# A decoder step with retrieved experts: the start of its first stream is rearranged (top-k of head groups as asides between the dots, scores in pairs, second trunk from pick 36)

## The chip, the cores and the metric

The kernel runs on one core of one Trainium2 chip. The metric is the device time of one execution in microseconds (us). A core has a matrix engine (TensorE, PE in the profile), a vector engine (VectorE, DVE), an engine for activations (ScalarE, ACT), GpSimd (POOL) and SyncE (SP). Each runs its own list of instructions in order. They wait for each other through semaphores, and 16 DMA engines move the data.

## The reference, cut to what matters

Two groups of tokens (512 prompt tokens and 8 sequences of 8 tokens) pass through two layers. A layer adds a mixer, a cross attention and a retrieval of experts ("PEER") to its input. Everything is float32. Only the last part matters for the change:

```python
q = einsum('td,de->te', t, w_pq).reshape(T, 8, 2, 128)        # 8 heads, two halves of a query
s = einsum('thpk,hpnk->thpn', q, sub_keys)                     # 128 scores for each half
s1, i1 = top_k(s[:, :, 0], 16);  s2, i2 = top_k(s[:, :, 1], 16)
cand = s1[..., :, None] + s2[..., None, :]                     # sums of the best of both halves
top_s, pos = top_k(cand, 16)                                   # 16 experts of 16384, for each head
g = softmax(top_s)
a = gelu(einsum('td,ted->te', t, peer_u[idx]))                 # a dot product with each expert's u row
out = einsum('te,ted->td', g * a, peer_v[idx])                 # a weighted sum of the v rows
```

Each token takes 128 experts (8 heads of 16), and each expert has a u row and a v row of 4 KB. The rows are gathered from memory.

## The kernel before

**Passes and picks.** Tokens lie in five tiles: four of 128 tokens, one of 64. A pass is one layer over one group of tiles: passes 0 and 2 take tiles 0 and 1, passes 1 and 3 take tiles 2 to 4. Each pass has a *trunk* (mixer, attention, queries and scores of the retrieval) and a *stream* of *picks*. A pick is one expert for each of the 128 tokens of a tile: one gather of 128 u rows (0.52 MB) and one of 128 v rows. Pass 0 has 256 picks (128 for each tile, head by head, 16 to a head), pass 1 has 320, and there are 1152 picks in all. While the stream of one pass runs, the trunk of the next pass is computed beside it.

**The order of the work.** It is fixed at build time by *steps*. Step m of the stream does the dot product of pick m (VectorE, `dot`, line 1793) and, `LAG` = 8 steps later, its weighted sum. The sum of a pick is done on VectorE (`sum_up`, line 1809) or on TensorE, as a product with a diagonal matrix of weights (line 1057); the first 40 picks of pass 0 are all summed on TensorE. `places` gives each trunk job the step at which it is due (`AHEAD`) and after which it may begin (`STARTS`). On each engine a function `peer_to(n)` first does all of that engine's stream work up to step n. TensorE calls it at the end of each job, with the next job's `STARTS`, and does the sums of picks m with m + 8 < n there. ScalarE calls it before it empties a job's result out of PSUM, and makes there, four picks at a time, gelu, weight (which needs the head's softmax factor, `gate`) and the diagonals. VectorE calls it before each piece of trunk work.

**GpSimd's queue** (`gather`, line 989) issues the gathers in one order. There are 8 buffers for u rows and 8 for v rows. The u row of pick m waits for the dot of pick m-8 and for its head's indices (`idx_done`). The v row of pick v waits for the sum of pick v-8. Before: the u rows of picks 0 to 7, then one wait for the attention's last product (its weights lie in the v buffers), then the v rows 0 to 7 in a burst, then u rows 8 to 15 alone, and from pick 16 on the u row of pick m and the v row of pick m-8 by turns.

**The start of the first stream.** Tile 0 of pass 0 is asked head by head. `first_tail` computes the queries and scores of heads 0 and 1 for both tiles, and the queries of head 2. After that the remaining columns of the query projection (jobs `pq`, two to a head, line 1084) and the scores (jobs `sc`, line 1399) follow in the order pq 6, 7, sc 2, pq 8, 9, sc 3, and so on to sc 7, with the steps 5, 11, 15, 19, 24, 29 for sc 2 to 7. The weights of `pq` come in four units of 2 MB into two slots, each loaded by SP when the unit before it in the slot is spent. SP loads the vectors of pass 1 (`PAR` and others) once sc 7 is done.

`top_group(0, k)` finds the experts of group k of the heads on VectorE; the groups are heads 0 | 1 | 2, 3 | 4, 5 | 6, 7. It has nine parts, and between two parts `breathe` calls `peer_to`, which spreads the dots over the group's window of steps. The windows are (0, 0), (0, 11), (11, 19), (19, 29), (29, 40). All five are run in line: VectorE waits at the start of each group for ScalarE to have copied its scores, and does no dot while it waits. Part 8 ends with the indices (line 1927). After part 9 `weigh_group` normalises the `gate` of the group before. `top_k(p, i)` for the other tiles runs as an *aside*: `peer_to` looks after each step whether the next part is due (`aside_to`). The trunk of pass 1 begins on all engines at step `FIRST` = 40 and is spread evenly to step 200.

Of the kernel before, what the change touches and what calls it, by code (L numbers as in the profile page):

```python
# [42 lines left out]
BLK = 4  # L43
# [9 lines left out]
FIRST = 40  # L53
HEAD = 40
# [87 lines left out]
def first_tail():  # L142

    jobs = [(at[:-1], "dve" if at[0] == "xo" else "act", 2 if at[0] in ("xo", "sk", "n") else 1, 1) for at in FIRST_TAIL]
    for h in range(2, PH):
        jobs += [(("pq", c), "act", 1, 1) for c in queries_before(h)] + [(("sc", h), "act", 2, 1)]
    return jobs
# [102 lines left out]

def places(p):
# [4 lines left out]
    if p == 0:  # L256
        score = {("sc", h): (0, 0, 5, 11, 15, 19, 24, 29)[h] for h in range(PH)}
# [5 lines left out]
    begin, end = step_base(p - 1) + (FIRST if p == 1 else LAG + 2), step_base(p)  # L263
# [179 lines left out]
def decoder_step(nc, A, O):  # L443
# [21 lines left out]
    with ExitStack() as ctx:  # L465
# [312 lines left out]
        def head_window(p, k):  # L778

            ends = [AHEAD[p, "sc", h + n - 1] for h, n in head_groups(p)] + [FIRST if p == 0 else step_base(p) + CARRY if carries(p) else step_base(p) - OVER]  # L780
# [186 lines left out]
        def _(pool):  # L967
# [31 lines left out]
            for m in range(STEPS_IN_ALL):  # L999
                if m == NU:  # L1000
                    pool.wait_ge(job_done, JOB[0, "xo", 1] + 1)
                    for v in range(NV):
                        gather_values(v)
# [6 lines left out]
                if m >= LAG + NV:  # L1010
# [4 lines left out]
        def _(pe):  # L1015
# [186 lines left out]
            def trunk(p):  # L1202
# [188 lines left out]
                for h in range(0 if p else 2, PH):  # L1391
                    for c in queries_before(h):
# [18 lines left out]
        def _(act):  # L1411
# [52 lines left out]
            asides += [(step_base(1) - 8, copy_beside, ())]  # L1464
            asides.sort(key=lambda a: a[0])
# [64 lines left out]
            def trunk(p):  # L1530
# [55 lines left out]
                n = ncols(g)  # L1586
                if p:
                    act.wait_ge(idx_done, turns_to(p - 1, len(GROUPS[(p - 1) % 2]) - 1 if g == 0 else 0))
                for a in range(2):
                    for c in range(BLK * a, BLK * a + BLK):  # L1590
                        evac((p, "c", c), F1[:, c, 0:n], pf((p, "c", c)))
                    for c in range(BLK * a, BLK * a + BLK):
                        evac((p, "u", c), F2[:, c, 0:n], pf((p, "u", c)), ACT.Gelu_apprx_tanh)
# [123 lines left out]
                for h in range(0 if p else 2, PH):  # L1717
                    for c in queries_before(h):
# [8 lines left out]
                    for k, (h0, some) in enumerate(head_groups(p)):  # L1727
                        if k and h == h0 + some - 1:
                            group_exps(p, k - 1)
                k = len(head_groups(p)) - 1  # L1730
                peer_to(head_window(p, k)[1] - 1)
                group_exps(p, k)
# [13 lines left out]
        def _(dve):  # L1746
# [95 lines left out]
            asides, going = [(p, i) for p in range(2 * DEPTH) for i in range(1, len(GROUPS[p % 2]))], []  # L1842

            def aside_to(n):

                while asides:
                    p, i = asides[0]
                    if not going:
                        going.append([0, top_k(p, i)])
                    k, work = going[0]  # L1850
                    if topk_steps(p, i, k) > n:
# [145 lines left out]
            def top_group(p, k):  # L1997
# [3 lines left out]
                first, after = head_window(p, k)  # L2001
                at = [0]

                def breathe():
                    at[0] += 1
                    peer_to(first + round((after - first) * at[0] / SEGS))

# [15 lines left out]
                breathe()  # L2023
# [4 lines left out]
                breathe()  # L2028
                each(lists, lambda a: dve.max_index(i16[:, a, 8:16], m16[:, a, 8:16], part[a]))
                candidates(all_cand, h, n)  # L2030
                breathe()
                each(heads, lambda a: dve.max(tops[:, a, 0:8], cand[a]))
                each(heads, lambda a: dve.max_index(pos[:, a, 0:8], tops[:, a, 0:8], cand[a]))
                breathe()
                each(heads, lambda a: dve.match_replace(cand[a], tops[:, a, 0:8], cand[a], LOWEST))
                each(heads, lambda a: dve.max(tops[:, a, 8:16], cand[a]))
                breathe()
# [3 lines left out]
                breathe()  # L2041
                marks = mark_table(S[0][:, h * 256:(h + n) * 256])
                ch.link(mark_places(marks, h, n))
                breathe()
                ch.link(mark_keys(marks, h, n))
                breathe()
# [3 lines left out]
                breathe()  # L2050
                if k and not carries(p):
                    weigh_group(p, k - 1)

            def trunk(p):
# [41 lines left out]
                peer_to(AHEAD[p, "par"])  # L2096
                for part in range(len(norm_parts(p, 0))):
# [203 lines left out]
                for i in range(nt):  # L2301
# [4 lines left out]
                    if i and not p:  # L2306
                        top_group(0, 0)
# [7 lines left out]
                for k in range(0 if p else 1, len(head_groups(p))):  # L2315
                    top_group(p, k)
                weigh_group(p, len(head_groups(p)) - 1)
# [47 lines left out]
```

## Time and profile before

| | us |
|---|---|
| time before, median of 3 runs (4105.68 to 4110.06) | 4108.83 |
| the profiled execution | 4111.88 |
| its span in the trace | 4110.0 |
| GpSimd busy / VectorE busy / TensorE busy | 2604.4 / 2929.3 / 3273.3 |

The span runs from the first to the last instruction, and 1.88 us of the profiled execution lie around it. The span has two parts. Up to 436.71 us the trunk of pass 0 runs alone. From there to the end the gathers run without a break of more than some 15 us. In the windows below, "DMA share" is the mean busy share of 16 DMA engines (1.03 is what a full stretch shows), and GB/s is what they moved.

### The profile page before, as it was taken

Reading aid. Unit: us, or ns where it says so; the run is one execution under the profiler, and the core shown is the slowest. Engines: PE = TensorE matmul, PEld = TensorE weight load, DVE = VectorE, ACT = ScalarE, POOL = GpSimd, SP = SyncE. Lnnn points to the kernel's source line nnn. Section 1 sums busy time; section 2 is a strip of 40 time slices with the busy share of each in tenths; the row PEclk is TensorE's granted clock in tenths of the full one; section 3 lists DMA queues with packets and bytes.
Section 4 is the critical chain, followed back from the end, with each engine's and each line's share of the span. In section 5 each row is a group of like instructions: output and inputs, shape, how many; then the busy total and the mean of one; then the engine's idle time right before and its main releaser. Section 6 shows DMA issues by size and latency. Waiting matters only on the chain. (4 is left out here: it accounts for less than half of the span.)

```text
span 4110.0 us, 37140 instructions
## 1 busy us (share of the span) xinstructions
PE 3273.3 (80%) x11224; PEld 1943.7 (47%) x11224; DVE 2929.3 (71%) x5930; ACT 1011.5 (25%) x2939; POOL 2604.4 (63%) x2318
## 2 busy tenths in 40 slices
PE   9999989898789788875848769897868866756666
PEld 6876646665546235664335426564635422212211
DVE  2110589988667878887776789997868776676754
ACT  1001331122422322122223421121313222321233
POOL 0000476676567677787777776777647777777775
PEclk9999999999889899887878969898879989988876
DMA  5445799999999999999999999999999999999998
GB/s 214 153 144 194 261 344 386 377 397 406 377 391 407 384 402 405 402 404 407 410 404 395 407 373 377 404 403 406 409 403 367 393 409 409 407 411 409 409 410 347
DMA packets 462382, 1522.37 MB, mean 370 GB/s; under 512 B 41220, under 2 KB 45604, under 8 KB 462184
## 3 DMA queue, kind: packets, MB, share of 16 engines
q0 software_dynamic: 331776, 1208.11, 74.9%
q1 hardware_dynamic: 130408, 311.90, 20.2%
q8 instruction: 91, 1.49, 0.1%
q14 instruction: 107, 0.88, 0.1%
HBM read 1512.62 MB, written 7.23 MB: 370 GB/s over the span
## 5 line engine op out<-in xcount | busy, mean ns | idle before, releaser
L989 POOL DMA_INDIRECT urow<-in_peer_u_dram,idx x1152 | 1323.3, 1149 | 1051.4 <-DVE idx L1927 440.8
L989 POOL DMA_INDIRECT vrow<-in_peer_v_dram,idx x1152 | 1278.8, 1110 | 437.5 <-issue 316.3
L1057 PE MATMUL ps<-vrow,diag 128*128 128x512 f32 (+1 forms) x2068 | 987.7, 694 | 393.8 <-DMA vrow<-in_peer_v_dram,idx 344.9
L1084 PE MATMUL ps<-RH,W 128*128 128x256 f32 (+1 forms) x4544 | 1174.5, 420 | 120.2 <-DMA W<-in_w_in_dram 46.2
L1084 PEld LDWEIGHTS ps<-RH,W 128*128 128x128 f32 x4544 | 892.0, 198 | 409.9 <-issue 96.3
L1793 DVE CUSTOM_DVE_ANT_0 urow<-urow,T 128x1024 f32<-128x1024 f32 x712 | 869.5, 1224 | 200.4 <-DMA urow<-in_peer_u_dram,idx 152.3
L1809 DVE SCALAR_TENSOR_TENSOR X<-vrow,wts,X 128x1024 f32<-128x1024 f32 x590 | 759.3, 1287 | 114.9 <-issue 95.8
L1057 PEld LDWEIGHTS ps<-vrow,diag 128*128 128x128 f32 (+1 forms) x2068 | 332.1, 195 | 998.5 <-issue 792.3
L1793 DVE CUSTOM_DVE_ANT_0 urow<-urow,ps 128x1024 f32<-128x1024 f32 x376 | 456.4, 1218 | 282.4 <-DMA urow<-in_peer_u_dram,idx 277.8
L1488 ACT ACTIVATE gel<-dots 128x4 f32<-128x4 f32 x288 | 59.0, 205 | 1782.3 <-DVE dots L1793 1759.0
L1084 PE MATMUL ps<-RB,W 128*128 128x256 f32 (+1 forms) x1024 | 253.4, 408 | 6.8 <-DVE RV L2232 3.1
L1506 ACT ACTIVATE diag<-ident,wts 128x128 f32<-128x128 f32 (+1 forms) x645 | 224.5, 372 | 127.3 <-PE ps L1057 123.3
L1490 ACT ACTIVATE wts<-gel,gate 128x1 f32<-128x1 f32 x1152 | 245.1, 283 | 9.3
L1084 PEld LDWEIGHTS ps<-RB,W 128*128 128x128 f32 x1024 | 195.3, 191 | 62.5 <-DVE RV L2232 3.5
L1106 PE MATMUL ps<-W,RV 128*128 128x512 f32 (+1 forms) x320 | 130.9, 613 | 54.1 <-DVE RV L2232 54.1
L1106 PE MATMUL ps<-W,RB 128*128 128x512 f32 (+1 forms) x384 | 162.1, 619 | 4.8 <-DVE RB L2155 3.1
L1106 PE MATMUL ps<-W,RH 128*128 128x512 f32 (+1 forms) x320 | 132.2, 610 | 17.4 <-DVE RH L2084 16.3
L1106 PEld LDWEIGHTS ps<-W,RV 128*128 128x128 f32 (+1 forms) x320 | 54.4, 186 | 128.6 <-issue 73.2
L1488 ACT ACT_TABLE_LOAD x76 | 97.5, 1283 | 66.1 <-issue 52.4
L1106 PEld LDWEIGHTS ps<-W,RB 128*128 128x128 f32 (+1 forms) x384 | 67.6, 190 | 96.9 <-issue 92.4
L1528 ACT ACTIVATE RB<-ps 128x256 f32<-128x256 f32 (+2 forms) x130 | 51.0, 418 | 249.4 <-PE ps L1084 221.1
L1528 ACT ACTIVATE RV<-ps 128x320 f32<-128x320 f32 (+4 forms) x110 | 47.9, 447 | 261.5 <-PE ps L1084 202.4
(271 smaller groups left out, 2309.0 us busy)
## 6 DMA issues: line engine op xcount, KB each, us to landing
W<-in_w_in_dram SPq DMA_DIRECT2D x56, 2048.0 KB, 18.6
W<-in_w_pq_dram SPq DMA_DIRECT2D x16, 2048.0 KB, 18.8
urow<-in_peer_u_dram,idx POOLq DMA_INDIRECT x1152, 15.1
vrow<-in_peer_v_dram,idx POOLq DMA_INDIRECT x1152, 15.2
W<-in_w_a_out_dram SPq DMA_DIRECT2D x8, 2048.0 KB, 19.1
W<-in_w_b_out_dram SPq DMA_DIRECT2D x8, 2048.0 KB, 19.2
W<-in_w_mix_o_dram SPq DMA_DIRECT2D x8, 2048.0 KB, 14.1
W<-in_w_xq_dram SPq DMA_DIRECT2D x8, 2048.0 KB, 18.9
```

Source lines behind the costliest of these rows:

```text
L989: return pool.indirect_dma_start(ring[:, slot, :], None, table, bass.IndirectOffsetOnAxis(ap=idx[:, q % TSLOT, e:e + 1], axis=0))
L1057: o = pe.matmul(out, diag[:, pe_turn[m] % NDIAG, 0:rows], vrow[:, m % NV, b * 512:(b + 1) * 512], start=m in pe_first, stop=m in pe_last)
L1084: m = pe.matmul(pf(name), slot(u)[:, k, c % BLK * P:c % BLK * P + P], src[:, k, 0:ncols(name[0] % 2)], start=(k == 0), stop=(k == KC - 1))
L1106: m = pe.matmul(out, src[:, k, i * P:i * P + rows], row_slot((p, kind, n))[:, k % 4, a * 512:(a + 1) * 512], start=(k == 0), stop=(k == KC ...
L1488: ch.link(act.activation(gel[:, :], dots[:, at, :], ACT.Gelu_apprx_tanh))
L1490: w = act.activation(wts[:, at, j:j + 1], gel[:, j:j + 1], ACT.Copy, scale=gate[:, q % TSLOT, e + j:e + j + 1])
L1506: made = act.activation(diag[part, pe_turn[m] % NDIAG, 0:rows], ident[part, part], ACT.Copy, scale=wts[part, m // GRP % WRING, m % GRP:m % ...
L1528: act.activation(out, in_, func).then_inc(act_evac, 1)
L1793: dve.tensor_tensor_reduce(urow[:, m % NU, :], urow[:, m % NU, :], rows, 1.0, 0.0, ALU.mult, ALU.add, dots[:, n % WRING, m % GRP:m % GRP + ...
L1809: dve.scalar_tensor_tensor(out=out, in0=vrow[:, m % NV, :], scalar=wts[:, m // GRP % WRING, m % GRP:m % GRP + 1], in1=base, op0=ALU.mult, ...
```

## The change

The change does six things. All but the last two concern the steps 0 to 46 of pass 0.

1. The groups 2, 3 and 4 of tile 0 become asides with windows of their own; the groups 0 and 1 stay in line. Group 1's window ends at step 8 (was 11).
2. The query columns come four at a time before two heads' scores: pq 6, 7, sc 2, sc 3, pq 8 to 11, sc 4, sc 5, pq 12 to 15, sc 6, sc 7. The scores' steps become 5, 5, 12, 12, 18, 18, so that TensorE has fewer sums to do ahead of them.
3. GpSimd issues u and v rows by turns from pick 8 on.
4. ScalarE's exponentials of a group become asides too, and the last group's gate is normalised at its own end.
5. The window of `top_k` of tile 1 moves from steps (40, 104) to (46, 106).
6. The trunk of pass 1 begins at step `SECOND` = 36 instead of 40. VectorE waits there for sc 7 to have been copied. The end of the trunk's stretch (step 200) stays.

```diff
+SECOND = 36
+FIRST_WINDOWS = ((0, 0), (0, 8), (12, 23), (23, 34), (34, 44))
+INLINE = 2
...
-    return step_base(p) + FIRST, step_base(p) + FIRST + WIDE
+    return step_base(p) + FIRST_WINDOWS[-1][1] + 2, step_base(p) + FIRST + WIDE + 2
...
+def queries_of(p, h):
+    if p:
+        return queries_before(h)
+    return () if h % 2 else tuple(range(2 * h + (2 if h == 2 else 0), 2 * h + 4))
...
-        score = {("sc", h): (0, 0, 5, 11, 15, 19, 24, 29)[h] for h in range(PH)}
+        score = {("sc", h): (0, 0, 5, 5, 12, 12, 18, 18)[h] for h in range(PH)}
...
-    begin, end = step_base(p - 1) + (FIRST if p == 1 else LAG + 2), step_base(p)
+    begin, end = step_base(p - 1) + (SECOND if p == 1 else LAG + 2), step_base(p)
...
             for m in range(STEPS_IN_ALL):
-                if m == NU:
+                if m == LAG:
                     pool.wait_ge(job_done, JOB[0, "xo", 1] + 1)
-                    for v in range(NV):
-                        gather_values(v)
...
-                if m >= LAG + NV:
+                if m >= LAG:
                     gather_values(m - LAG)
...
+            asides += [(first + (after - first) * 6 // SEGS + 1, group_exps, (0, k)) for k, (first, after) in enumerate(FIRST_WINDOWS) if k]
...
+            asides[:0] = [(0, -k) for k in range(INLINE, len(FIRST_WINDOWS))]
+            def aside_steps(p, i, k):
+                if i > 0:
+                    return topk_steps(p, i, k)
+                first, after = FIRST_WINDOWS[-i]
+                return first + round((after - first) * k / SEGS)
...
-                breathe()
+                yield
...
+                if p == 0 and k == len(FIRST_WINDOWS) - 1:
+                    weigh_group(p, k)
+            def heads_inline(p, k):
+                first, after = head_window(p, k)
+                for at, part in enumerate(top_group(p, k)):
+                    peer_to(first + round((after - first) * (at + 1) / SEGS))
...
+                if p == 1:
+                    await_evac(dve, LAST_SC[0])
```

## Rows read from the trace of the kernel before

**Rows 1.** The page: DMA's share in 40 slices; the sums on VectorE (busy, mean ns).

```profile
DMA 5445799999999999999999999999999999999998
...
L1809 DVE SCALAR_TENSOR_TENSOR X<-vrow,wts,X 128x1024 f32<-128x1024 f32 x590 | 759.3, 1287 | 114.9 <-issue 95.8
```

**Rows 2.** Windows: stretch, its length, PE, PEld, DVE, ACT, POOL busy, PEclk, DMA share, GB/s.

```profile
440.00:545.00 105.00, 90.43 (x392) 66.32 (x392) 67.08 (x232) 32.75 (x98) 59.68 (x56) 0.95 0.97 360
545.00:656.00 111.00, 101.56 (x319) 50.68 (x318) 92.46 (x262) 35.43 (x98) 88.64 (x73) 0.97 0.97 356
656.00:870.00 214.00, 200.86 (x749) 141.51 (x749) 210.33 (x442) 36.66 (x106) 137.12 (x111) 0.95 1.00 381
...
860.00:880.00 20.00, 17.71 (x66) 12.24 (x66) 18.23 (x25) 6.21 (x14) 16.57 (x12) 1.00 1.03 403
```

**Rows 3.** Waits of POOL, 440 to 545 us: for whom, us in total, times, longest.

```profile
POOL vrow L989 <- PE ps L1057: 23.8, 7, 5.8
POOL urow L989 <- DVE idx L1927: 7.2, 1, 7.2
```

**Rows 4.** Timeline of POOL: start, us, instruction, [idle before it, and its releaser].

```profile
468.92 0.94 POOL L989 DMA_INDIRECT urow<-in_peer_u_dram,idx  x1 [0.30 <-issue]
...
484.57 0.94 POOL L989 DMA_INDIRECT vrow<-in_peer_v_dram,idx  x1 [5.79 <-PE ps L1057]
...
526.86 0.94 POOL L989 DMA_INDIRECT vrow<-in_peer_v_dram,idx  x1 [3.64 <-PE ps L1057]
...
537.62 1.07 POOL L989 DMA_INDIRECT vrow<-in_peer_v_dram,idx  x1 [0.30 <-issue]
...
544.71 0.94 POOL L989 DMA_INDIRECT vrow<-in_peer_v_dram,idx  x1 [4.77 <-PE ps L1057]
```

**Rows 5.** Timeline of VectorE around the indices of head 1.

```profile
455.39 1.23 DVE L1793 CUSTOM_DVE_ANT_0 urow<-urow,T 128x1024 f32<-128x1024 f32 x1
...
472.34 1.23 DVE L1793 CUSTOM_DVE_ANT_0 urow<-urow,T 128x1024 f32<-128x1024 f32 x1 [15.71 <-DMA urow<-in_peer_u_dram,idx]
...
476.66 0.17 DVE L1927 SCALAR_TENSOR_TENSOR idx<-RB 128x16 uint32<-128x16 uint16 x1
```

**Rows 6.** Timeline of TensorE from pq 8 on (a job's matmuls are recorded twice).

```profile
469.06 8.83 PE L1084 MATMUL ps<-RH,W 128*128 128x256 f32 x32 [2.75 <-DMA W<-in_w_pq_dram]
...
482.35 5.39 PE L1057 MATMUL ps<-vrow,diag 128*128 128x512 f32 x12 [3.56 <-ACT diag L1506]
487.57 7.07 PE L1084 MATMUL ps<-RH,W 128*128 128x256 f32 x32
...
540.39 0.34 PE L1073 MATMUL ps<-ident,PAR 48*128 48x48 f32 x1 [6.04 <-DMA PAR<-in_conv_w_dram]
540.66 24.94 PE L1057 MATMUL ps<-vrow,diag 128*128 128x512 f32 x52
```

**Rows 7.** Timeline of ScalarE: the wait for head 0's gate, and a group's exponentials.

```profile
478.33 1.28 ACT L1488 ACT_TABLE_LOAD   x1 [12.50 <-DVE gate L1995]
...
485.07 1.28 ACT L1426 ACT_TABLE_LOAD   x1
486.37 0.31 ACT L1426 ACTIVATE gate<-tops,gneg 128x16 f32<-128x16 f32 x1
```

**Rows 8.** Windows, columns as in rows 2: three thinner stretches of the DMA.

```profile
600.00:620.00 20.00, 20.00 (x55) 8.16 (x54) 18.70 (x45) 2.11 (x10) 15.97 (x14) 1.00 0.93 328
800.00:820.00 20.00, 17.75 (x56) 12.22 (x57) 19.48 (x35) 4.06 (x8) 13.51 (x10) 0.79 0.84 297
...
1040.00:1080.00 40.00, 32.09 (x203) 25.74 (x201) 31.55 (x44) 23.45 (x48) 17.51 (x14) 0.87 0.86 337
```

**Rows 9.** Timeline of SP's queue from 600 us: the weight loads of pass 1.

```profile
618.14 147.23 SPq L951 DMA_DIRECT2D W<-in_w_in_dram  x9
```

**Rows 10.** Waits of all engines, 1000 to 1100 us.

```profile
DVE rmax L2257 <- PE ps L1300: 18.3, 1, 18.3
...
PE ps L1073 <- DVE RB L2076: 6.8, 1, 6.8
```

More of the change, by code:

```diff
@@ L145, in first_tail @@
     for h in range(2, PH):
-        jobs += [(("pq", c), "act", 1, 1) for c in queries_before(h)] + [(("sc", h), "act", 2, 1)]
+        jobs += [(("pq", c), "act", 1, 1) for c in queries_of(0, h)] + [(("sc", h), "act", 2, 1)]
     return jobs
@@ L778, in head_window @@
         def head_window(p, k):
-            ends = [AHEAD[p, "sc", h + n - 1] for h, n in head_groups(p)] + [FIRST if p == 0 else step_base(p) + CARRY if carries(p) else step_base(p) - OVER]
+            if p == 0:
+                return FIRST_WINDOWS[k]
+            ends = [AHEAD[p, "sc", h + n - 1] for h, n in head_groups(p)] + [step_base(p) + CARRY if carries(p) else step_base(p) - OVER]
             return ends[k], ends[k + 1]
@@ L1391, in trunk @@
                 for h in range(0 if p else 2, PH):
-                    for c in queries_before(h):
+                    for c in queries_of(p, h):
                         project((p, "pq", c), c, hT)
@@ L1586, in trunk, with evac_gated @@
                 n = ncols(g)
+                def evac_gated(some):
+                    for c in some:
+                        evac((p, "u", c), F2[:, c, 0:n], pf((p, "u", c)), ACT.Gelu_apprx_tanh)
                 if p:
@@ L1591, in trunk @@
                         evac((p, "c", c), F1[:, c, 0:n], pf((p, "c", c)))
-                    for c in range(BLK * a, BLK * a + BLK):
-                        evac((p, "u", c), F2[:, c, 0:n], pf((p, "u", c)), ACT.Gelu_apprx_tanh)
+                    evac_gated(range(BLK * a, BLK * a + BLK))
                 if g:
@@ L1717, in trunk @@
                 for h in range(0 if p else 2, PH):
-                    for c in queries_before(h):
+                    for c in queries_of(p, h):
                         evac((p, "pq", c), qp[c // 2 % 3][:, c % 2, 0:n], pf((p, "pq", c)))
@@ L1727, in trunk @@
                     for k, (h0, some) in enumerate(head_groups(p)):
-                        if k and h == h0 + some - 1:
+                        if p and k and h == h0 + some - 1:
                             group_exps(p, k - 1)
-                k = len(head_groups(p)) - 1
-                peer_to(head_window(p, k)[1] - 1)
-                group_exps(p, k)
+                if p:
+                    k = len(head_groups(p)) - 1
+                    peer_to(head_window(p, k)[1] - 1)
+                    group_exps(p, k)
             for p in range(2 * DEPTH):
@@ L2314, in trunk @@
                     dve.sem_inc(row_spent, 1)
-                for k in range(0 if p else 1, len(head_groups(p))):
-                    top_group(p, k)
-                weigh_group(p, len(head_groups(p)) - 1)
+                for k in range(0 if p else 1, len(head_groups(p)) if p else INLINE):
+                    heads_inline(p, k)
+                if p:
+                    weigh_group(p, len(head_groups(p)) - 1)
             ch.mark(dve.memset(eps[:, :], EPS))
```

27 lines of the change are left out of this document (11 added, 16 removed).

## The prediction

> **What bounds the kernel now.** I read the page first, then the windows, the waits of GpSimd, and the timelines of the first 110 us of the stream.
>
> The page shows no engine above 80% busy, but the DMA engines stand at full share in nearly every slice after the fourth [rows 1]. A full stretch shows a share of 1.03 and 403 GB/s [rows 2]. The bytes are fixed, so after the stream's start the end moves only by what the DMA leaves unused. I count that as (403 - rate)/403 of a stretch. It is 11.2 us in 440 to 545 (360 GB/s), 12.9 us in 545 to 656 (356) and 11.7 us in 656 to 870 (381) [rows 2]. Later there are 6.6 us in 1040 to 1080 (337) [rows 8]. The change touches nothing else, since passes 2 and 3 keep their steps.
>
> Each of these stretches has its own limit. In 440 to 545 GpSimd waits 23.8 us in 7 waits for TensorE's sums, and 7.2 us once for VectorE's indices [rows 3]. In 545 to 656 it issues 73 gathers, two to a step: 111/36.5 = 3.04 us a step. In 656 to 870 VectorE is busy for 210.33 of 214 us [rows 2].
>
> **The wait for head 1's indices goes (edit 1, with 3).** Before, group 1's window of 11 steps puts dots 8 and 9 ahead of the indices. Dot 8 waits 15.71 us for its row, because the v rows 0 to 7 were queued ahead of it, so the indices come at 476.66 [rows 5] and GpSimd idles 7.2 us for them [rows 3]. Now only dots 0 to 6 stand ahead. Dot 7 is done at 456.6 [rows 5], so the indices come at about 458 and the gate of head 0 at about 459. The u row of pick 16 goes out at 470, when the 24 gathers ahead of it are issued [rows 4]. Taken alone that is worth 7 us.
>
> **What is late next (edit 2).** The next gather is v row 8, and it needs sum 0. Before, sum 0 follows sc 3; now it follows sc 4. ScalarE's 12.50 us wait for the gate goes too [rows 7], but it was not last: TensorE is held by its own products. I count from 469.06, where the weights of pq 8 arrive; that load is not moved. Pq 8 and 9 take 8.83, pq 10 and 11 another 6.9 (one pair is 7.07 with its tail), sc 4 1.05: 485.8 [rows 6]. Sum 0 takes 1.8 (5.39/3) and v row 8 goes at 487.9, against 484.57 [rows 4]. Between sum 0 and sum 3 ScalarE now makes head 1's exponentials and switches its table twice (1.28 + 0.5 for the first [rows 7], 1.28 + 1.1 for gelu and weights), so sum 3 ends at 493.3 instead of 491.3 or so.
>
> Now the queue behind: sc 5 to 494.3, pq 12 to 15 in 13.9 to 508.2, sc 6 to 509.2, and only then sums 4 to 9 (10.8) to 520.0, sc 7 to 521.0. So v row 12 waits from about 497 to 511, a stall of 14 us where before there were several of 4 to 6. Behind v row 12 stand all later u rows in GpSimd's queue. SP loads `PAR` after sc 7, and TensorE stood 6.04 us for it [rows 6]: 527.1, against 540.39. From there to the gather that the first sum releases took 4.3 us before (540.39 to 544.71) [rows 6, 4], which gives v row 18 at 531.4. Four pairs of gathers took 537.62 - 526.86 = 10.76, or 2.69 a pair [rows 4], so v row 24 goes at 531.4 + 6 x 2.69 = 547.5. Before it went at 544.71 [rows 4].
>
> The start of the stream therefore brings **+2.8 us**. The removed index wait is eaten by the sums. The bounds are -11.2 (the DMA full throughout) and +16.1 (the third rival).
>
> A rule of the Trainium skill (ScalarE: Activation LUTs, What ACT_TABLE_LOAD costs) puts a switch of the table at 1.28 us plus 1.38 us of drain. The trace shows 485.07 to 486.37, so 1.30 to the next instruction [rows 7], and no drain. By the page sum 3 would end up to 2.8 us later. Nothing else hangs on that.
>
> **The head groups as asides, ScalarE's exponentials, VectorE's wait for sc 7.** The same instructions run, the same number of times. Dots no longer wait for ScalarE's copies. But GpSimd waited for a dot nowhere in 440 to 545 [rows 3], so this is free, and bounded by the 12.9 us that lie unused in the next stretch. I take 0. Sc 7 is done 35 us ahead of step 36, so the new wait costs nothing.
>
> **The trunk of pass 1 from step 36.** Four steps of 3.04 us are 12.2 us; less the 2.8 the trunk starts 9.4 us earlier. Its first weight load after the two already there is at 618.14 [rows 9] and comes at about 608.7. In 600 to 620 the DMA leaves 3.7 us unused (328 GB/s) [rows 8], of which 11.3/20 lie behind 608.7: **-2.1 us** (bounds 0 and -3.7).
>
> From 656 VectorE sets the pace. At step s the trunk is now at (s - 36)/164 of its way instead of (s - 40)/160, which is 2.1% further at step 62 (the step near 656 us). The stretch has 55.5 steps of about 2.5 us for a dot (1.23 [rows 5]) and a sum (1.29 [rows 1]), so some 70 us of VectorE's 210 are trunk and tile 1's top-k, over 37% of the trunk's way. 2.1% of 70/0.37 is 4.0 us that is already done when VectorE becomes the limit. I take **-3.5**, near that end, because VectorE has 3.7 us of slack in all [rows 2]. The bounds are -5, and +3 where tile 1's top-k, two steps later, falls on the trunk's gating; the thinnest stretch, 297 GB/s in 800 to 820, leaves 5.3 us [rows 8].
>
> At 1046 VectorE stands 18.3 us for the attention scores [rows 10], and this makes the 6.6 us unused in 1040 to 1080. It lies in TensorE's products between the second norm and the scores, and before them TensorE waits 6.8 us for VectorE's norm [rows 10]: a head start of TensorE ends in that wait. The steps between are 2.5% more per product. I take **-1** (bounds -6.6 and +1).
>
> The sum is +2.8 - 2.1 - 3.5 - 1.0 = -3.8. The profiled execution took 4111.88 (its span of 4110.0 and 1.88 around it), which gives 4108.1. It stands 3.05 above the median of the runs, so against that median I forecast 4108.8 - 3.8 = 4105.0.
>
> **The rivals.** *The start is fed after all.* If v rows 8 to 17 are not held by sums 0 to 9 (pq 8 to 11 quicker, or loads of weights filling the gap), the 11.2 us go in full: -11.2 - 2.1 - 1 = -14, or 4094.5. For it: 31 us of GpSimd's idle time in that stretch [rows 3], and the loads of pass 1's first weights come forward by 11 us, since the first of them waits for pq 11. Against it: TensorE is busy 90.43 of 105 us [rows 2], and no product goes.
>
> *The head start carries through.* TensorE and its weight loads are the trunk's limit right up to the scores, the norm's 6.8 us wait notwithstanding, and the 18.3 us wait shrinks by 9: -6.6 in place of -1, so -9.4, or 4099.4. For it: TensorE is busy 94% of 656 to 870 [rows 2]. Against it: that wait of 6.8.
>
> *Slower: the ring of v rows starves.* Each microsecond by which the sum after `PAR` is later than 527 holds GpSimd for a microsecond, because v row 18 and everything behind it wait. If sc 7 or the load of `PAR` comes no earlier than before (TensorE at its lower clock, as in pq 8 and 9, or `PAR` queued behind the second weight load), v row 18 goes at 544.7 and v row 24 at 560.8: +16.1 in place of +2.8. The loads of pass 1's weights fill some of such a gap, so I take half way, +9.4, for its price, and 4108.8 + 9.4 = 4118.2 where the earlier trunk then brings nothing. It decides from a `PAR` transposition later than 530, where the term reaches +5.7 and outweighs the later ones but for 1 us. For it: TensorE's order puts six sums behind four products, and the stall near 500 is certain to come. Against it: TensorE had 12.4 us of waits in that stretch (2.75, 3.56 and 6.04 [rows 6]), and one of them goes.
>
> *It does nothing.* The terms cancel, VectorE's relief falls where the DMA is full anyway (1.03 in 860 to 880 [rows 2]): 4108.8.
>
> **How the numbers follow.** About 8 us (0.2%) is what a measurement can tell from no change. Forecast 0.43 (its own range 4101 to 4109), start fed 0.19, head start carries 0.13, starved 0.19, nothing 0.06. Faster by over 8.2 us (below 4100.6): the first rival, two thirds of the second and a rest of the forecast, 0.19 + 0.09 + 0.05 = 0.33. Slower: most of the third and a rest of the others, 0.19. The same: 0.48. The range of 4092 to 4117 takes in the first rival and reaches to the third; it leaves out 0.1 on either side.
>
> **What would show it.** Right: GpSimd's wait for `idx` near 477 is gone; v row 8 goes at about 488; one long stall ends near 511; sc 7 near 521, `PAR`'s transposition near 527, v row 24 between 545 and 550; the load of 618.14 near 609; the 18.3 us wait before 1046 nearly as long. Wrong: DMA above 385 GB/s in 440 to 545, or that wait under 12 us (faster rivals); `PAR` transposed after 530 or a new wait of GpSimd for `idx` (slower). The prediction fails as a whole if the time leaves the range, or if it moves by stretches behind 1250 us, which the change doesn't touch.

## The result

The changed kernel takes 4120.92 us (median of 12 runs, 4116.86 to 4125.27), the kernel before on the same chip 4109.49 (12 runs, 4104.11 to 4119.41). The ratio is 1.0029, with an interval of 1.0022 to 1.0036. So it is slower by some 11 us, where 4 us faster were forecast, and it lies above the range. The profiled execution took 4119.95 with a span of 4117.9, 7.9 longer than before.

**The start of the stream came nearly as predicted.** Of GpSimd's timeline, the gathers that waited, up to 545 us (start, us, instruction, idle before it):

```profile
487.68 0.94 POOL L1001 DMA_INDIRECT vrow<-in_peer_v_dram,idx  x1 [16.74 <-PE ps L1067]
...
510.26 0.94 POOL L1001 DMA_INDIRECT vrow<-in_peer_v_dram,idx  x1 [12.96 <-PE ps L1067]
...
529.98 0.94 POOL L1001 DMA_INDIRECT vrow<-in_peer_v_dram,idx  x1 [4.00 <-PE ps L1067]
```

Of TensorE's timeline, score 7 and the transposition of `PAR`, and of SP's queue the weight load that stood at 618.14:

```profile
518.41 1.05 PE L1409 MATMUL ps<-KV,RV 128*128 128x128 f32 x8
525.66 0.34 PE L1083 MATMUL ps<-ident,PAR 48*128 48x48 f32 x1 [6.20 <-DMA PAR<-in_conv_w_dram]
```

```profile
614.10 21.32 SPq L963 DMA_DIRECT2D W<-in_w_in_dram  x2
```

The wait for `idx` [rows 3] is gone, v row 8 goes at 487.68 (487.9 predicted), the long stall ends at 510.26 (511), and `PAR` is transposed at 525.66 (527.1).

**The loss stands at 656 to 700 us.** The windows of the kernel after (stretch, length, busy time of PE, PEld, DVE, ACT and POOL, PEclk, DMA share, GB/s); the first three lines answer to the first three of [rows 2], the fourth to the first of [rows 8]:

```profile
440.00:545.00 105.00, 95.50 (x393) 69.09 (x394) 61.92 (x218) 33.38 (x102) 56.37 (x53) 0.93 0.91 344
545.00:656.00 111.00, 100.32 (x322) 50.01 (x320) 82.42 (x223) 32.59 (x84) 75.31 (x69) 0.97 0.97 366
656.00:870.00 214.00, 201.29 (x745) 141.77 (x745) 208.93 (x472) 35.76 (x102) 135.43 (x110) 0.96 0.95 360
...
600.00:620.00 20.00, 20.00 (x54) 7.83 (x53) 15.12 (x39) 0.85 (x4) 9.57 (x9) 1.00 0.81 294
...
656.00:700.00 44.00, 44.00 (x159) 30.77 (x159) 42.54 (x112) 2.11 (x10) 18.93 (x14) 0.96 0.77 286
670.00:680.00 10.00, 10.00 (x39) 7.04 (x38) 9.47 (x20) 0.00 (x0) 3.31 (x3) 1.00 0.36 119
```

The window from 656 to 700 of the kernel before:

```profile
656.00:700.00 44.00, 44.00 (x166) 31.17 (x166) 42.71 (x105) 2.11 (x10) 18.06 (x15) 0.96 1.00 384
```

Counted as in the prediction, (403 - rate)/403 of the stretch, 44 us at 286 GB/s leave 12.8 us unused and at 384 GB/s 2.1: 10.7 us more, in one hole. The other stretches add up to little. The first 105 us lose 4.2 more (344 against 360). The next 111 gain 2.8 (366 against 356), and 656 to 870 as a whole loses 11.2 (360 against 381). That is 12.6. Less the 2.85 by which the first gather went earlier (433.86 against 436.71) it is 9.7. The change did not bring these 2.85: a second trace of the kernel before (e9) has its first gather at 434.15. The u row of pick 256, far behind all this, went out at 1368.9 against 1360.3, 8.6 us late. The spans differ by 7.9, so little is given back or lost after it.

The clock of TensorE is no part of it: the granted clock is 0.96 in 656 to 700 in both kernels, and 1.00, its upper level, in the 56 us ahead.

**What makes the hole.** Waits of VectorE, 545 to 720 us (for whom, us in total, times, longest), after:

```profile
DVE bns L2152 <- ACT RV L1578: 11.2, 2, 10.5
DVE urow L1809 <- PE ps L1130: 9.2, 1, 9.2
```

and before, the wait of the same place:

```profile
DVE urow L1793 <- PE ps L1120: 4.6, 1, 4.6
```

L1578 is ScalarE's gelu of the v projection, L1130 (before, L1120) the spread of lg and lb on TensorE. Spread after and before, in TensorE's timelines:

```profile
652.36 3.83 PE L1130 MATMUL ps<-GV,ident 16*128 16x128 f32 x32
```

```profile
653.82 3.83 PE L1120 MATMUL ps<-GV,ident 16*128 16x128 f32 x32
```

VectorE's consumer of the spread is due three picks earlier (58 for lg instead of 61), and VectorE comes to it 6.1 us earlier (654.45 - 9.25 = 645.20, against 655.91 - 4.59 = 651.32, from its timelines). TensorE has it ready only 1.5 us earlier. The reason stands in TensorE's timeline of the v projection (L1116), which began 7.8 us earlier (589.29 against 597.11) and ended 0.6 earlier (635.01 against 635.61):

```profile
589.29 5.39 PE L1116 MATMUL ps<-W,RH 128*128 128x512 f32 x12 [2.57 <-DVE RH L2109]
594.52 1.88 PE L1067 MATMUL ps<-vrow,diag 128*128 128x512 f32 x4
596.23 3.60 PE L1116 MATMUL ps<-W,RH 128*128 128x512 f32 x8
...
619.25 1.88 PE L1067 MATMUL ps<-vrow,diag 128*128 128x512 f32 x4
620.96 14.05 PE L1116 MATMUL ps<-W,RH 128*128 128x512 f32 x40
634.94 17.49 PE L1094 MATMUL ps<-RH,W 128*128 128x320 f32 x64
```

TensorE takes the row sums up to step 48 (`head_steps`). With the trunk begun at 36, six of them fall between the products of the v projection, at 1.72 us each (594.52 to 596.23); before there were two. Those four take 6.9 of the 7.8 us. VectorE now stands 10.5 us for the gelu (to 625.65) and 9.2 for the spread (to 654.45).

GpSimd waits for the sums that now lie in the projection as well, four times between 604 and 622 us, where before it waited for nobody from 600 to 656. The DMA ran at 294 GB/s in 600 to 620 (328 before [rows 8]). Of GpSimd's waits, 600 to 656 us:

```profile
POOL vrow L1001 <- PE ps L1067: 10.3, 4, 3.3
```

While VectorE stands for the spread it makes no dot, so no u row comes free, and GpSimd waits again (timeline of GpSimd, 648 to 676 us):

```profile
648.83 0.94 POOL L1001 DMA_INDIRECT vrow<-in_peer_v_dram,idx  x1 [0.30 <-issue]
655.95 1.74 POOL L1001 DMA_INDIRECT urow<-in_peer_u_dram,idx  x1 [6.18 <-DVE dots L1809]
...
662.42 1.18 POOL L1001 DMA_INDIRECT vrow<-in_peer_v_dram,idx  x1 [0.30 <-issue]
674.23 1.74 POOL L1001 DMA_INDIRECT urow<-in_peer_u_dram,idx  x1 [10.63 <-DVE dots L1809]
```

The second wait is VectorE's product with lg and lb, nine instructions without a dot. It was there before too (9.26 us), but then the buffers were full when it began: six gathers had gone out in the 9.5 us before the wait, now four in 14 us. Two stands in a row empty the queues, and 119 GB/s at 670 to 680 is the result (406 before).

### The profile page after: what moved, and what is told of

It reads as the page before. It is cut to its first block and busy times, and to the rows that moved or that the text cites. A ratio compares the mean times of both kernels' runs of the same rounds, so it can differ in the third digit from the quotient of the medians.

```text
span 4117.9 us, 37139 instructions
## 1 busy us (share of the span) xinstructions
PE 3266.8 (79%) x11224; PEld 1935.1 (47%) x11224; DVE 2930.0 (71%) x5930; ACT 1012.1 (25%) x2939; POOL 2602.7 (63%) x2318
## 5 line engine op out<-in xcount | busy, mean ns | idle before, releaser
L1116 PE MATMUL ps<-W,RV 128*128 128x512 f32 (+1 forms) x320 | 131.8, 616 | 62.7 <-DVE RV L2259 62.7
L1116 PE MATMUL ps<-W,RB 128*128 128x512 f32 (+1 forms) x384 | 159.5, 612 | 6.2 <-DVE RB L2182 3.1
L1116 PE MATMUL ps<-W,RH 128*128 128x512 f32 (+1 forms) x320 | 130.4, 602 | 18.8 <-DVE RH L2109 18.3
L1116 PEld LDWEIGHTS ps<-W,RV 128*128 128x128 f32 (+1 forms) x320 | 54.7, 187 | 137.8 <-issue 73.7
L1116 PEld LDWEIGHTS ps<-W,RB 128*128 128x128 f32 (+1 forms) x384 | 66.5, 187 | 96.7 <-issue 91.3
L1809 DVE CUSTOM_DVE_ANT_0 urow<-urow,RV 128x1024 f32<-128x1024 f32 x64 | 78.2, 1225 | 43.5 <-DMA urow<-in_peer_u_dram,idx 41.2
## 6 DMA issues: line engine op xcount, KB each, us to landing
W<-in_w_mix_o_dram SPq DMA_DIRECT2D x8, 2048.0 KB, 14.3
```

What stands on the lines that cost most here:

```text
L1116: m = pe.matmul(out, src[:, k, i * P:i * P + rows], row_slot((p, kind, n))[:, k % 4, a * 512:(a + 1) * 512], start=(k == 0), stop=(k == KC ...
L1809: dve.tensor_tensor_reduce(urow[:, m % NU, :], urow[:, m % NU, :], rows, 1.0, 0.0, ALU.mult, ALU.add, dots[:, n % WRING, m % GRP:m % GRP + ...
```

## The experiments

Each was timed in five rounds beside the kernel before. The first eight ran on two chips that took 3% longer for every kernel (4231.64 and 4246.88 us for the kernel before; DMA 374 to 376 GB/s in 3000 to 4000 us against 403), with more scatter: the time from the u row of pick 256 to the end, which the change doesn't touch, was between 2857 and 2877 us in their traces, and between 2747 and 2752 in all the others. The others ran where the kernel before took 4110 to 4112. So the sizes come from the later ones. The rate in brackets is the DMA's at 656 to 700 us. "After" is the changed kernel.

**The first batch: one part at a time.** e1 is after with

```diff
-SECOND = 36
+SECOND = 40
```

> The changed kernel with the trunk of pass 1 from step 40 again; all edits of steps 0 to 46 stay. Theory A (the trunk's due steps lie 4 steps earlier than TensorE can follow, so VectorE stands 10.5 us for the gelu of v and 9.2 us for the spread lg, lb, where before it stood 4.6): the long wait for the gelu goes, the wait for lg/lb falls under 6 us, DMA in 656 to 700 us is back above 370 GB/s (286 in the changed kernel), and the time falls by 6 to 10 us, to 0.1% of the kernel before. Rival B (the head of the stream costs it: v row 24 is 3.5 us later counted from the first gather, and VectorE without its backlog runs into the same waits anyway): the waits stay within 3 us of the changed kernel's, the time stays 0.2 to 0.3% above before.

e2 is after with VectorE's steps alone put off:

```diff
-                return AHEAD[name] + {"v": LATE_GELU, "oa": ...
+                return AHEAD[name] + {"v": LATE_GELU + 3, "lg": 3, "lb": 3, "oa": ...
```

> The changed kernel, trunk still from step 36, but VectorE takes v, lg and lb of pass 1 three steps later (steps 56, 61 and 63 in place of 53, 58 and 60); no other engine's list changes. Theory A: VectorE does dots while TensorE finishes, the two waits shrink from 19.7 us in all to under 10, and the time falls by 5 to 9 us. Rival B: no change, 0.2 to 0.3% above before. Rival C (TensorE is late because six sums in place of two now lie within its projection of v, and everything after it is late too): VectorE only waits later, at the short convolution, and under 3 us come back.

e3 is the kernel before with the trunk's start alone:

```diff
-    begin, end = step_base(p - 1) + (FIRST if p == 1 else LAG + 2), step_base(p)
+    begin, end = step_base(p - 1) + (36 if p == 1 else LAG + 2), step_base(p)
```

> The kernel before with the trunk of pass 1 planned from step 36; VectorE still runs the groups to step 40 in line, with nothing else of the change. Theory A: the cost comes with it, 0.12 to 0.3% slower than before, with VectorE's waits for the gelu of v and for lg/lb over 12 us in all. Theory D (it takes both: 36 hurts only where VectorE has no backlog of dots): within 0.1% of before. Rival B: within 0.05%.

e4 is after with the scores of one head at a time, as before:

```diff
-        score = {("sc", h): (0, 0, 5, 5, 12, 12, 18, 18)[h] for h in range(PH)}
+        score = {("sc", h): (0, 0, 5, 11, 15, 19, 24, 29)[h] for h in range(PH)}
-    return () if h % 2 else tuple(range(2 * h + (2 if h == 2 else 0), 2 * h + 4))
+    return queries_before(h)
```

> The changed kernel with the order of queries and scores of before (pq two at a time, scores at steps 5, 11, 15, 19, 24, 29) and the trunk from 36. The sums of the first picks come earlier: v row 8 near 477 in place of 487.7 us, no stall of GpSimd over 8 us behind it. If the head's cost of 3.5 us at v row 24 passes through, the time falls by 3 to 4 us against the changed kernel. If PAR is late again as before (540), v row 24 is where it was before and the waits of theory A shrink too, since TensorE's lateness is then shared by the stream: 0.1 to 0.2% above before. If nothing of the head passes through, it stays at 0.29%.

Measured: e1 1.0032 [1.0021, 1.0044], e2 1.0021 [1.0011, 1.0031], e3 1.0024 [1.0009, 1.0039], e4 1.0016 [1.0003, 1.0029]. e3 shows that the start from 36 makes a kernel slower without anything else of the change. Its trace has the same two waits as after and 289 GB/s at 656 to 700, on a trunk that is otherwise the old one:

```profile
DVE bns L2125 <- ACT RV L1567: 12.2, 1, 12.2
DVE urow L1793 <- PE ps L1120: 12.1, 1, 12.1
```

e1 seems to speak against this: its trace has no wait for the gelu and the u rows up to pick 80 go out 12 us earlier than in after, yet its median is as bad. But its traced execution was the fastest of its eight, at 4233.59 us, 2 us above the median of the kernel before on that chip. The trace shows no loss because that execution had hardly any. What the other seven lost, and where, is open.

e2 does not decide. Its ratio lies between what theory A and rival C asked for, its interval overlaps that of after, and its trace still has a wait of 7.3 us ahead of a dot and 326 GB/s at 656 to 700. In e4 v row 8 goes at 478.61, near the 477 expected, but both waits stay as in after (10.0 and 9.2 us) and so does the rate behind them (285 GB/s). What the start of the stream gains there does not reach the hole.

**The second batch: a control, the start of the trunk on the other side, the two parts together.** e5 is the changed kernel as it is, e6 is e1 again, e7 has `SECOND = 44`, and e8 is e4 with `SECOND = 40`.

> The changed kernel again, beside the kernel before, as the control of the following three. All theories: 0.22 to 0.36% slower than before; the u row of pick 70 is issued about 27 us later than before, counted from the first gather, and that of pick 256 about 11.

> The trunk from 40 again, as in e1, whose trace showed the early loss gone (u row of pick 70 at 225 us after the first gather, before 224, changed 251) while its time was no better. Theory A: the time is 0.1 to 0.25% below the control's. Rival E (what the early stretch gives is lost again later, where the DMA limits): equal to the control within 0.05%, and the u row of pick 256 is no earlier than in the control.

> The changed kernel with the trunk of pass 1 from step 44. Theory A: VectorE's waits for the gelu and for lg/lb shrink further (under 5 us in all), the u row of pick 70 comes at 222 us or less after the first gather, and the time lies 0.2 to 0.35% below the control's, so within 0.1% of before. Rival F (a later trunk is denser and lost in 656 to 1100 us): u row of 256 no earlier than with 40.

> Order of queries and scores of before and the trunk from 40; groups as asides, gathers by turns. e4 showed the u row of pick 50 at 156 us after the first gather, against 164 before. Theory A: the trunk's wait for TensorE eats part of it, the u row of pick 70 comes near 222 to 226, and the time is within 0.1% of before, 0.2 to 0.3% below the control. If the 8 us carried through it would be 0.15 to 0.2% faster than before.

Measured: e5 1.0039 [1.0023, 1.0055], e6 1.0013 [0.9998, 1.0029], e7 1.0044 [1.0030, 1.0057], e8 1.0004 [0.9990, 1.0018]. The control confirms the loss. With 40 more than half of it goes by the medians, though the intervals of e5 and e6 overlap, and with the old scores too, nearly all. The u row of pick 70 came 236 to 240 us after the first gather in e6, e7 and e8, later than the 222 to 226 expected. And 44 was not expected to be slow: starting later is no cure in itself. Its hole lies earlier and has another face. Windows and GpSimd's timeline of e7:

```profile
600.00:656.00 56.00, 48.76 (x144) 22.39 (x145) 47.07 (x121) 5.53 (x19) 47.21 (x24) 0.90 0.68 245
```

```profile
615.62 9.85 POOL L1001 DMA_INDIRECT urow<-in_peer_u_dram,idx  x1 [0.31 <-issue]
625.78 0.94 POOL L1001 DMA_INDIRECT vrow<-in_peer_v_dram,idx  x1 [0.30 <-issue]
627.02 7.56 POOL L1001 DMA_INDIRECT urow<-in_peer_u_dram,idx  x1 [0.31 <-issue]
```

GpSimd waited for nobody there; single gathers lasted up to 9.85 us in place of 0.94. In addition the first weight load of this stretch began only at 635.87, so nothing else was there to fill the queues.

**The third batch: a null, the best start, the asides alone, fewer sums on TensorE.** e9 is the kernel before; e10 has `SECOND = 38`; e11 is e8 with GpSimd's first value rows in a burst behind pick 13, as before, which leaves of the change the asides, with their windows and ScalarE's part in them (parts 1, 4 and 5):

```diff
-                if m == LAG:
+                if m == NU:
                     pool.wait_ge(job_done, JOB[0, "xo", 1] + 1)
+                    for v in range(NV):
+                        gather_values(v)
-                if m >= LAG:
+                if m >= LAG + NV:
```

e12 is after with TensorE's sums up to step 44 in place of 48:

```diff
-    return (FIRST + LAG, 2 * HEAD, 0, 0)[p]
+    return (SECOND + LAG, 2 * HEAD, 0, 0)[p]
```

> The kernel before itself, for what a comparison of equals gives on this kernel and for its trace on a chip of this batch. All theories: ratio 1.000, within 0.001 of it; stream 700 us on as in the other kernels of the batch. If it comes out at 1.0013 or more, the differences of 0.13 to 0.16% that single parts of the change showed are not shown at all, and only the 0.39% of the whole change is.

> The changed kernel with the second trunk from pick 38. Theory A (the trunk's VectorE steps are due earlier than TensorE can have its results ready, so VectorE stands at the spread of lg and lb, GpSimd gets no row freed and the queues run dry at 656 to 700 us): ratio between that of 40 (1.0013 and 1.0032) and of 36 (1.0039), about 1.003, and a wait for the spread of lg and lb between 9 and 12 us. Theory F (there is a best place between two holes, since 44 was slower too): 1.001 or less, less than with 40. Theory B (the start of the stream is the cause): as with 36, 1.0035 to 1.004.

> The changed kernel with the second trunk from pick 40, the scores of one head at a time as before, and GpSimd's first value rows in a burst behind pick 13 as before: of the change only the top-k of head groups as asides is left. Theory A (the later start of the trunk's VectorE work and the order of the scores hold all of it): ratio 1.000, within 0.001. Rival C (the asides between the dots delay the last head group or the first dots of the trunk): 1.001 to 1.002, with the loss in the stretch 430 to 600 us.

> The changed kernel with 44 instead of 48 as the step up to which TensorE takes the row sums, so that four sums fewer stand within the v projection; trunk from pick 36 kept. A sum took TensorE 1.72 us there (594.52 to 596.23), four take 6.9 us; VectorE gets four sums of 1.27 us, 5.1 us. Theory A: TensorE has lg and lb about 6 us earlier (spread at 646 to 648 instead of 652), VectorE's wait for them falls from 9.2 to 1 to 4 us, GpSimd's gap of 7.1 us at 649 to 656 goes, DMA at 656 to 700 us over 340 GB/s, ratio 1.0015 to 1.0025 against 1.0039 of the control. Theory B (start of the stream, order of the scores): all of the loss stays, 1.0035 to 1.0045, whatever happens at 650. Rival D (VectorE's own work bounds this stretch, not TensorE): the wait goes and VectorE is full, the hole is as large as before, 1.004 or more.

Measured: e9 0.9998 [0.9989, 1.0007], e10 0.9995 [0.9986, 1.0004], e11 1.0004 [0.9995, 1.0013], e12 1.0016 [1.0007, 1.0025]. The null is a null (397 GB/s). The asides cost nothing that can be measured. Two picks of a later start bring back all 11 us (332 GB/s): e10 differs from after in `SECOND` alone, and the intervals lie apart. This was expected of theory F, not of theory A. So both sides of a best place are real. The hole at 656 to 700 has not gone in e10, but it is paid for: in 600 to 656 the DMA ran at 403 GB/s (372 before, 365 after). VectorE's waits in e10 are both shorter than in after:

```profile
DVE urow L1809 <- PE ps L1130: 6.7, 1, 6.7
DVE bns L2152 <- ACT RV L1578: 3.7, 1, 3.7
```

In e12, still from 36, the wait for the gelu nearly goes (0.6 us) and half of the loss with it. TensorE's spread moves to 648.25, as expected. The wait for it stays at 9.3, which was not expected: VectorE, no longer held by the gelu, comes to it earlier as well. Nor was the rate of 301 GB/s at 656 to 700, where over 340 was expected.

**The fourth batch.** e13 is e10 with `head_steps` as in e12 (step 44), e14 is e10 with the old scores, e15 is e7 with TensorE's sums up to step 56.

> Second trunk from pick 38 and TensorE's row sums up to step 44 instead of 48: four sums fewer (6.9 us) in the v projection. Theory A (what counts is how long VectorE stands for lg and lb, and so how long no row is freed): VectorE's wait for the spread, 6.7 us with 38 alone, falls to 0 to 4 us, DMA at 656 to 700 us from 332 to 360 to 390 GB/s, ratio 0.998 to 0.9995. Rival D (the sums that VectorE takes over cost it as much as the wait they save): wait shorter but VectorE later, 0.9995 to 1.001.

> Second trunk from pick 38 with the scores of one head at a time as before; GpSimd's early value rows and the asides kept. If the new order of the scores costs something of its own at the start of the stream (the value row 24 came 112.5 us after the first gather with it, 105 to 108 us without): ratio 0.998 to 0.9993. If what the start of the stream wins or loses is levelled by the hole at 656 to 700 us: as with 38 alone, 0.9990 to 1.0005.

> Second trunk from pick 44 (which alone gave 1.0044, with 245 GB/s at 600 to 656 us) and TensorE's row sums up to step 56 instead of 48: eight sums of 1.27 us, 10.2 us, leave VectorE, 13.8 us come to TensorE. Theory G (VectorE works off a backlog of dots and sums back to back there, GpSimd's gathers last up to 9.85 us beside it, so the queues run dry): the gathers of 9.85 and 7.56 us go or shrink below 4 us, DMA at 600 to 656 us above 320 GB/s, ratio 1.001 to 1.0025. Theory A alone (TensorE late): VectorE then stands 10 us and more for gelu or lg and lb, ratio 1.004 or more, with the hole at 656 to 720 us.

Measured: e13 0.9991 [0.9982, 1.0000], e14 0.9991 [0.9982, 1.0000], e15 1.0039 [1.0026, 1.0053] (five executions). e14's 0.9991 lies in both of its expected ranges and decides nothing. e13 is the cleanest case for the mechanism. Its spread, its wait for it, and its DMA:

```profile
645.09 3.83 PE L1130 MATMUL ps<-GV,ident 16*128 16x128 f32 x32
```

```profile
DVE urow L1809 <- PE ps L1130: 0.7, 1, 0.7
```

```profile
656.00:700.00 44.00, 40.87 (x146) 28.32 (x145) 42.85 (x117) 2.11 (x10) 21.70 (x18) 0.96 1.03 400
```

The wait has gone, and the hole with it. In e15 the gathers of 9.85 and 7.56 us are gone (the longest after 600 us lasts 3.93), as theory G had it, but the DMA at 600 to 656 rises only to 302 GB/s and the time does not move. TensorE's sums came behind the v projection, and a value row waited for one:

```profile
659.00 0.94 POOL L1001 DMA_INDIRECT vrow<-in_peer_v_dram,idx  x1 [13.62 <-PE ps L1067]
```

VectorE stood 6.7 us for the gelu and 6.2 for the spread, below the 10 that theory A alone asked for. So at 44 one engine's lateness was traded for the other's, and neither theory holds by itself.

**The last batch.** e16 joins what helped: trunk from 38, sums up to 44, old scores. e17 is the kernel before with the sums up to 44 and nothing else.

> Second trunk from pick 38, TensorE's row sums up to step 44, scores of one head at a time as before; early value rows and asides kept. With the hole at 656 to 700 us closed (400 GB/s, 0.9991), the start of the stream is the next loss: value row 24 came 111.2 us after the first gather with the scores of two heads together and 105.6 us with the old order. If it counts: 5 us less than 0.9991, 0.9975 to 0.9985. If it is levelled again behind: 0.9985 to 0.9995.

> The kernel before with TensorE's row sums up to step 44 instead of 48, nothing of the change. VectorE's wait for lg and lb there was 4.6 us with 384 GB/s behind it (2.8 us and 397 GB/s in a second trace), and of the four sums two stood in the v projection, 3.4 us. Theory A: little to gain, 0.9990 to 1.0000. If the four sums alone are what made 38 with 44 good: 0.9991 or less, the same as e13.

Measured: e16 4102.35 us against 4109.93, 0.9980 [0.9971, 0.9989]; e17 1.0011 [1.0002, 1.0020]. e16 beats both kernels, by 7.6 us and by some 20. Its gain does not come from a closed hole:

```profile
656.00:700.00 44.00, 44.00 (x165) 31.02 (x165) 42.88 (x116) 2.11 (x10) 22.62 (x19) 1.00 0.90 320
```

The shift of the sums alone makes the kernel before slower: it brings back stretched gathers (6.36 us at 603.11) and 331 GB/s at 600 to 656, while VectorE's wait for the spread, 4.6 us before, is gone. So the four sums alone are not what made e13 fast. That VectorE's four more sums stretch the gathers is likely and not shown.

**All traces on the faster chips.** The waits are VectorE's for the gelu and for the spread (us in total, 545 to 720), the rates are GB/s, and the last column is when the u row of pick 80 went out, in us after the first gather.

| | trunk from, sums to | scores | ratio | waits | 600 to 656 | 656 to 700 | pick 80 |
|---|---|---|---|---|---|---|---|
| before | 40, 48 | old | 1 | 0, 4.6 | 372 | 384 | 275.7 |
| e9 | 40, 48 | old | 0.9998 | 0, 2.8 | 375 | 397 | 276.6 |
| e17 | 40, 44 | old | 1.0011 | 0, 0 | 331 | 403 | 281.3 |
| after | 36, 48 | new | 1.0029 | 11.2, 9.2 | 365 | 286 | 289.3 |
| e12 | 36, 44 | new | 1.0016 | 0.6, 9.3 | 383 | 301 | 281.4 |
| e10 | 38, 48 | new | 0.9995 | 3.7, 6.7 | 403 | 332 | 276.6 |
| e14 | 38, 48 | old | 0.9991 | 7.6, 6.7 | 366 | 336 | 274.8 |
| e13 | 38, 44 | new | 0.9991 | 0, 0.7 | 397 | 400 | 270.5 |
| e16 | 38, 44 | old | 0.9980 | 0, 4.4 | 394 | 320 | 270.6 |
| e11 | 40, 48 | old | 1.0004 | 1.1, 12.1 | 373 | 328 | 278.0 |
| e15 | 44, 56 | new | 1.0039 | 7.4, 6.2 | 302 | 369 | 287.2 |

Neither a single wait nor a single window orders the times: e11 stands 12.1 us for the spread and e14 14.3 us in all, and neither is slower than before. The u row of pick 80, 705 to 724 us into the span, does follow them, to about 3 us (e15, which loses 5 us more behind it, at 367 GB/s in 700 to 870 against 380). So nearly all that these kernels gain or lose is made before it. What a stand of a given length costs there is open.

## Why the prediction was wrong

**The start of the stream: right.** It was +2.8. By the unused DMA 440 to 545 lost 4.2. V row 24 went 111.5 us after the first gather where it had been 108.0, 3.5 later. That it went at 545.38, near the 544.71 of before and under the 547.5 predicted, is owed to the first gather, which was 2.85 us earlier; over all traces it goes at 433.84 to 437.12, whatever the kernel. The mechanism (the index wait goes, the sums behind four products take its place) held step by step. By the Trainium skill (ScalarE: Activation LUTs, What ACT_TABLE_LOAD costs), with its drain, sum 3 would have ended up to 2.8 us behind the 493.3 predicted; it ended at 492.67 (485.45 and 7.22), so the trace goes with the duration that was read from the row.

**The trunk's loads: right in size by luck.** -2.1 was predicted, from 600 to 620 us, and 545 to 656 gained 2.8. But 600 to 620 ran at 294 GB/s against 328 and lost 1.7. The load came at 614.10, not at 609: 4.0 us earlier instead of 9.4, because it waits for the first half of the v projection, in which four sums now lay where there had been two. The gain was made ahead of it:

```profile
545.00:600.00 55.00, 46.38 (x139) 22.23 (x138) 46.46 (x153) 23.69 (x67) 44.64 (x35) 0.93 0.94 340
545.00:600.00 55.00, 44.32 (x131) 20.65 (x130) 47.34 (x141) 21.90 (x60) 43.41 (x39) 0.94 0.98 368
```

The first line is before, the second after, 3.8 us less unused. The prediction put the asides at 0 there. The three traces without asides have 322 to 340 GB/s in this window, and the eight with them have 353 to 378 (e11, with little else of the change, 353).

**VectorE's relief from 656: this step failed, with its sign.** The prediction gave -3.5, bounds -5 and +3; measured, the stretch lost 11.2, of it 10.7 in its first 44 us. The step took a fraction of VectorE's work as "already done when VectorE becomes the limit", as if the trunk were VectorE's alone. What VectorE does of a trunk waits for TensorE and ScalarE, and it waits in the same queue as the dots. TensorE was full ahead of it, also in the kernel before:

```profile
600.00:656.00 56.00, 55.18 (x181) 28.45 (x180) 46.00 (x110) 11.73 (x31) 44.01 (x39) 1.00 0.99 372
```

From 585 us to the end of the v projection it makes seven sums in both kernels; of these two lay within the projection before, and six after. So the projection began 7.8 us earlier and ended 0.6 earlier. In place of work done early there came 20 us of standing. (Its size was also worked out from too large a part of the trunk: 55.5 of 160 steps are 35% and not over 37%, which makes the 4.0 us 4.2 and changes nothing.) It was readable beforehand: the wait of 4.6 us for L1120 stood in the trace of before, and would grow by what VectorE's step advanced and TensorE's did not. e3 shows the start from 36 alone slow, e10 shows two picks give the loss back, and e12 and e13 show that sums taken from TensorE give back half from 36, and close the hole from 38. How the loss divides between VectorE's two stands and GpSimd's waits for the sums is not shown.

**The scores' wait behind 1046: no gain.** -1 predicted; the wait was 19.2 us in place of 18.3, and 1000 to 1200 ran at 387 GB/s against 391 (2 us). The rival in which the head start carries through is out with it.

**The rivals.** The one that ended slower put the loss at the start, with `PAR` after 530; `PAR` came at 525.66. Its time, 4118.2, is near what was measured, by another mechanism, so that nearness is luck. The rival in which the start is fed asked for over 385 GB/s in 440 to 545; it was 344. A rival with VectorE waiting for TensorE in the moved trunk was not on the list.

**What the parts are worth.** The old order of the scores was the better in each of four pairs (e8 and e6 by 0.09%, e14 and e10 by 0.04%, e16 and e13 by 0.11%, e4 and e5 by 0.23% across two chips). Each pair's intervals overlap, so a gain of some 0.1% is possible and not shown. e16's 0.9980 lies in the range expected if the start counted, but the traces speak for levelled behind: v row 24 went 105.4 us after the first gather, in e13 111.2, but at pick 80 the two are level (270.6 and 270.5), and the traced execution of e16 took 4103.92 us, that of e13 4102.91.

**Open.** Why e1's median was at 1.0032 and e6's at 1.0013, one kernel on two slower chips; and what of e7's loss is stretched gathers and what the late weight load.

## What to carry to other kernels

Where one engine's queue holds both the work that frees buffers and the consumers of another engine's results, moving the consumers' due steps earlier only lengthens the wait, unless the producer has slack just there: read its busy share ahead of the consumer, and count what is interleaved with it. In these traces a single stand was paid for by full buffers; price the second one that follows before they have filled again. And a due step has a best place with a loss on either side (36 and 44 both cost 0.3 to 0.4% here, 38 and 40 nothing that can be told), so measure both neighbours before calling a direction good.

## What the hardware showed unexpectedly

GpSimd's gathers stretch beside VectorE. In e7 the gather of 615.62 lasted 9.85 us, to 625.47, while VectorE worked off a backlog of dots and sums back to back, all with two inputs from SBUF; it ended 0.9 us after VectorE turned at 624.58 to index searches. Two stretches of VectorE's timeline in e7:

```profile
615.22 1.21 DVE L1809 CUSTOM_DVE_ANT_0 urow<-urow,T 128x1024 f32<-128x1024 f32 x1
...
616.36 1.27 DVE L1825 SCALAR_TENSOR_TENSOR X<-vrow,wts,X 128x1024 f32<-128x1024 f32 x1
...
623.39 1.27 DVE L1825 SCALAR_TENSOR_TENSOR X<-vrow,wts,X 128x1024 f32<-128x1024 f32 x1
624.58 0.07 DVE L1979 MATCH_VALUE_LOAD i<-m,KV 128x8 f32 x1
624.65 0.28 DVE L1979 FIND_INDEX8 i<-m,KV 128x8 uint16<-128x128 f32 x1
```

The gather of 627.02 does the same: it ended at 634.58, 0.9 us after VectorE turned from six such instructions to index searches at 633.69. In the kernel before, a gather of 4.86 us (585.03) ended 0.9 us after VectorE turned from three dots to a search for maxima at 589.01. An undisturbed gather takes 0.94 us, so each looks as if it had been done only after the run.

Yet in after, the dot of 798.82 (1.25 us) follows straight behind a sum, and the gather of 798.81 beside it took 0.93; that of 800.05, beside the sum of 800.00, took 0.94. What decides between the two is open, and no run here was made for it. The Trainium skill (SBUF — State Buffer, SBUF: two separate sides) has a port pair that VectorE and GpSimd lock against each other for a whole instruction, with two-input operations in it only against a GpSimd operation that reads SBUF. The first case looks like such a lock, but held over eight instructions and not one; the last two gathers show none.
